# A decoder layer on one core: GpSimd's first row pass is moved behind the latents' inverse root and woven with weight splits, and three more weight loads stand ahead of it

## The chip, the cores and the metric

The kernel runs on one core of a Trainium2 chip. The metric is the device time of one execution in microseconds (us); lower is better. Engines are named as in the profile: PE is TensorE, PEld its weight loads, DVE is VectorE, ACT is ScalarE, POOL is GpSimd, SP is SyncE, which issues the DMAs.

## The reference

One post-norm decoder layer over 1024 tokens of width 1024, in float32. What this case touches is the start: the embedding LayerNorm and the first products with `w_in`.

```python
x = layer_norm(x, emb_ln_g, emb_ln_b)
proj = x @ w_in[l]
u_pool, q, c, iq, ik, iw = jnp.split(proj, SPLIT_POINTS, axis=-1)
pooled = causal_multiscale_pool(u_pool)
c = rms_norm(c, kv_norm_g[l])
o_lat = dsa_sparse_attention(q_lat, c, iq, ik, iw, rel_bias)   # indexer scores, top 256 keys, softmax
mix = jnp.concatenate([pool_out, attn_out], axis=-1) @ w_o[l]
x = layer_norm(ALPHA * x + mix, ln1_g[l], ln1_b[l])            # the residual is the normalized x
```

The normalized x is needed twice: transposed, as the operand of `w_in`, and by rows (with gain and bias), as the residual of the sum after the attention.

## The kernel before

All tokens are worked in two chunks of 512 (four blocks of 128 rows each, tile `rows`). Every product is exact to float32 by three passes: an operand is split in a high part (rounded to fp32r) and a low part (what is left), and PE adds high x high, low x high and high x low (lines 1427, 1428, 1429). The transposed x of a chunk is in `xhi` and `xlo`.

Weights come in units of 128 rows by 1024 columns. Unit n is loaded by SP into `wring[n % 4]`; ACT makes its high part `whi[n % 2]` (line 1133), as soon as PE is done with unit n - 2; POOL or DVE makes the low part `wlo[n % 2]` (`split_lo`, line 397); then PE multiplies. The units of chunk 0 are, in order, 0 ik, 1 c, 2 to 5 iq0 to iq3 (all split by DVE), and 6 to 9 u0 to u3, 10 to 13 q0 to q3 (split by POOL). SP may load unit n only when the low part of unit n - 4 is done, since both lie in one slot of the ring (line 415).

The order of each engine's work is written out by hand, and engines wait for one another by counting semaphores. What matters here:

- POOL: the rows' affine pass, `emb_gains` (lines 628 and 629): each of four blocks is multiplied by the gain and then gets the bias, and counts up `emb_rows`. Then `latents_inverse_rms` (lines 693 and 694), which waits for ACT's four sums of squares and which ACT waits for ahead of `lat_val`. Then the low parts of u0 to q1, and then, between the low parts of q2 and q3, the inverse roots for chunk 1 (lines 681 and 683), which wait for DVE's statistics.
- SP, one queue in program order: after the first loads, units 4 to 6; then it waits for each `emb_rows` and writes that block to memory (line 482); waits until all four are written; loads the x of chunk 1 over them (line 485); writes and reads back the bias rows (lines 488 and 490); then the units from 7 on.
- DVE: `x_lo` (lines 558 and 563), the low parts of c and iq0, `keys_queries_lo` (lines 588, 589, 599, 600, with the low parts of iq1 to iq3 between), then for each u unit the pooling (lines 529 to 548), for each unit two score sums (lines 859 and 863), and from the fourth unit on a block's statistics and normalization of chunk 1 (lines 814 to 828). After that comes `select_pair`, the top-k of two blocks (lines 879 to 890).
- ACT: for each unit `hi_after`, the high part of the unit two further on, and behind it in its queue the evacuation of this unit's product and two `relu_dots`. PE: the product of each unit (24 groups of matmuls of 512 columns) and two `dot`s; the first dot waits for the low parts of all four iq products.

Of the kernel before, what the change touches and what calls it, by code (L numbers as in the profile page):

```python
# [134 lines left out]
def layer(nc, x, emb_ln_g, emb_ln_b, rel_bias, w_in, pool_w, pool_scale, kv_norm_g, w_uk, w_uv, w_o,  # L135
# [15 lines left out]
    with ExitStack() as ctx:  # L151
# [195 lines left out]
        units = []  # L347
# [6 lines left out]
        U = {name: n for n, name in enumerate(units)}  # L354
# [37 lines left out]
        def split_lo(eng, name, sem_lo, at=None):  # L392

            n = U[name]

            eng.wait_ge(hi_ready, n + 1 if at is None else at)
            eng.tensor_tensor(parts_of(name, wlo[n % 2]), parts_of(name, wring[n % 4]),  # L397
                              parts_of(name, whi[n % 2]).bitcast(F32), ALU.subtract).then_inc(sem_lo, 1)
# [10 lines left out]
        def _(sp):  # L409
            def load_unit(name):  # L410
                n = U[name]
                slot = wring[n % 4]
                if n >= 4:

                    sp.wait_ge(*LO[units[n - 4]])
                if name[0] == "wo":
                    _, c, nh, u = name
                    sp.dma_start(k_pairs(slot), wod[:, 2 * u:2 * u + 2, nh * 512:nh * 512 + 512]).then_inc(ring_in[n % 4], 16)
                elif name[0] == "ik":

                    sp.dma_start(parts_of(name, slot), wind[:, :, COL_IK:COL_IK + KEYW]).then_inc(ring_in[n % 4], 16)
                else:
                    col = {"c": COL_C, "iq": COL_IQ, "q": COL_Q, "u": COL_U}[name[0]] + (P * name[2] if name[0] != "c" else 0)
                    sp.dma_start(k_columns(slot), wind[:, :, col:col + P]).then_inc(ring_in[n % 4], 16)

            def load_gains(g, b):
                sp.dma_start(gains[:, 0, :], g.to_broadcast([P, D])).then_inc(gains_in, 16)
                sp.dma_start(gains[:, 1, :], b.to_broadcast([P, D])).then_inc(gains_in, 16)
# [27 lines left out]
            def load_units(names):  # L456
                for name in names:
                    load_unit(name)
# [16 lines left out]
            sp.dma_start(wuv[:, :], w_uv.rearrange("o c h d -> (o c) (h d)")).then_inc(late_in, 16)  # L475
            sp.dma_start(poolw[:, :, :], pool_w.rearrange("o g c d -> c (o g) d")).then_inc(late_in, 16)
            load_gains(emb_ln_g.rearrange("(o d) -> o d", o=1), emb_ln_b.rearrange("(o d) -> o d", o=1))
            load_units(units[4:7])

            for b in range(CB):  # L480
                sp.wait_ge(emb_rows, b + 1)
# [2 lines left out]
            for b in range(CB):  # L484
# [4 lines left out]
            sp.wait_ge(bias_out, 16)  # L489
            sp.dma_start(near_up[:, :, :], bass.AP(tensor=bias_rows.tensor, offset=0, ap=[[1, P], [FWIN, HEADS], [1, NEAR]])  # L490
                         ).then_inc(bias_in, 16)
            load_units(units[7:U[("wo", 0, 1, 0)]])
            for b in range(CB):
                sp.wait_ge(emb_rows, CB + b + 1)
                sp.dma_start(spilld[CB + b], rows[:, b, :]).then_inc(spilled, 16)
# [127 lines left out]
        def emb_gains(eng, c, link):  # L623

            eng.wait_ge(gains_in, 32)
            eng.wait_ge(g_full, G[("xT", c, KT - 1)] + 1)
            for b in range(CB):
                link(eng.tensor_tensor(rows[:, b, :], rows[:, b, :], gains[:, 0, :], ALU.mult))
                eng.tensor_tensor(rows[:, b, :], rows[:, b, :], gains[:, 1, :], ALU.add).then_inc(emb_rows, 1)
                yield b  # L630
# [13 lines left out]
        def _(pool):  # L644
# [32 lines left out]
            def inverse_std(l, blocks=range(CB)):  # L677
                for b in blocks:
                    n = 4 * l + b
                    pool.wait_ge(stats_ready, n + 1)  # L680
                    pool.tensor_scalar(rstd[:, n:n + 1], mean_var[:, n, 1:2], EPS, None, ALU.add).then_inc(var_eps, 1)
                    pool.wait_ge(var_eps, n + 1)
                    pool.tensor_tensor(rstd[:, n:n + 1], rstd[:, n:n + 1], power[:, :], ALU.pow).then_inc(rstd_ready, 1)
                    if l in (LN1_0, LN1_1) or (l == LN2_1 and b in OUT_SHARED):
                        pool.wait_ge(rstd_ready, n + 1)
                        pool.tensor_scalar(shift[:, n:n + 1], mean_var[:, n, 0:1], rstd[:, n:n + 1], -1.0, ALU.mult, ALU.mult)\
                            .then_inc(shift_ready, 1)

            def latents_inverse_rms(c):
                at = slice(CB * c, CB * c + CB)  # L690

                pool.wait_ge(csum_ready, CB * c + CB)
                link(pool.tensor_scalar(crstd[:, at], csum[:, at], 1.0 / LAT, EPS, ALU.mult, ALU.add))
                pool.tensor_tensor(crstd[:, at], crstd[:, at], power[:, :].to_broadcast([P, CB]), ALU.pow)\
                    .then_inc(crstd_ready, 1)
# [38 lines left out]
            def lo(*names):  # L734
                for name in names:
                    split_lo(pool, name, lo_pool)

            inverse_std(EMB0)
            for b in emb_gains(pool, 0, link):
                pass  # L740
            latents_inverse_rms(0)
            lo(*units[U[("u", 0, 0)]:U[("q", 0, 2)]])

            inverse_std(EMB1, [0])
            lo(("q", 0, 2))
# [959 lines left out]
```

## Time and profile before

| what | value |
|---|---|
| median of 3 runs | 1308.09 us (1307.64 to 1311.28) |
| span of the profiled execution | 1309.0 us |
| PE busy | 1223.0 us (93%) |
| DVE busy | 869.9 us (66%) |
| ACT busy | 578.9 us (44%) |
| POOL busy | 539.0 us (41%) |

The page gives the profiled execution's span and no other time of it. The span is 0.9 us over the median of the three runs and inside their range. Busy shares are means over the whole program; the change lies in the first 130 us, where three engines hand work to one another, so the rows below are from there.

### The profile page before, as it was taken

The numbers are of one execution on the slowest core, as the hardware profiler recorded it, in microseconds if no ns is written. First come the engines' busy times: TensorE is split into PE (matmuls) and PEld (weight loads), VectorE is DVE, ScalarE is ACT, GpSimd is POOL, SyncE is SP. The second block draws the span as 40 slices with busy tenths as digits, with TensorE's granted clock in tenths as the row PEclk, the third lists the DMA queues.
The fourth block names the chain that finished last, engine by engine and source line by source line (L and its number), as shares of the span: only waits on it lengthen the run. The fifth ranks groups of instructions, "written<-read, shape, count | busy, mean of one in ns | idle before, by whom it ended". The sixth has DMA issues, their size and how long they took to land.

```text
span 1309.0 us, 17244 instructions
## 1 busy us (share of the span) xinstructions
PE 1223.0 (93%) x5639; PEld 981.3 (75%) x5639; DVE 869.9 (66%) x1322; ACT 578.9 (44%) x961; POOL 539.0 (41%) x390
## 2 busy tenths in 40 slices
PE   4999898799979999999999999989899999999994
PEld 2786685577868778778778698877688888888883
DVE  7577999765879888888888679833842232322345
ACT  3445642675564334243343376642542442433420
POOL 5434674422248666666665733214801102002004
PEclk9899999899989999999999999999799999999997
DMA  6722232131123232332322200403123323223331
GB/s 195 241 74 64 65 81 96 43 119 33 28 70 97 83 101 90 95 96 96 93 87 93 96 1 34 161 17 81 49 98 96 96 96 95 89 90 95 96 96 64
DMA packets 125723, 114.28 MB, mean 87 GB/s; under 512 B 5662, under 2 KB 99435, under 8 KB 125675
## 3 DMA queue, kind: packets, MB, share of 16 engines
q1 hardware_dynamic: 125674, 113.67, 28.0%
q8 instruction: 27, 0.44, 0.1%
q14 instruction: 22, 0.17, 0.0%
HBM read 105.25 MB, written 8.40 MB: 87 GB/s over the span
## 4 chain that ended last, share of the span: by engine, by line
PE 75%; DVE 14%; issue 6%; ACT 2%; POOL 1%; DVEq 1%; DMA 0%; ACTq 0%; POOLq 0%
PE g_bank L1427 14%; PE g_bank L1428 13%; PE g_bank L1429 13%; PE wide L1427 10%; PE wide L1429 10%; PE wide L1428 10%; PE g_bank L1401 2%; DVE logit L924 1%; DVE xlo L563 1%; DVE win L533 1%; PE wide L1530 1%; PE wide L1490 1%; PE wide L1489 1%; DVE probs_lo L940 1%; DVE score L863 1%
## 5 line engine op out<-in xcount | busy, mean ns | idle before, releaser
L397 POOL TENSOR_TENSOR wlo<-wring,whi 128x1024 fp32r<-128x1024 f32 (+1 forms) x102 | 252.4, 2476 | 274.1 <-ACT whi L1133 161.2
L1427 PE MATMUL g_bank<-xhi,whi 128*128 128x512 f32 (+1 forms) x736 | 298.5, 406 | 8.6 <-DVE xlo L563 5.8
L1313 ACT ACTIVATE whi<-wring 128x1024 fp32r<-128x1024 f32 x124 | 131.4, 1059 | 392.9 <-PE wide L1429 198.1
L1428 PE MATMUL g_bank<-xlo,whi 128*128 128x512 f32 (+1 forms) x736 | 294.5, 400 | 0.0
L1429 PE MATMUL g_bank<-xhi,wlo 128*128 128x512 f32 (+1 forms) x736 | 294.2, 400 | 0.0
L397 DVE TENSOR_TENSOR wlo<-wring,whi 128x1024 fp32r<-128x1024 f32 (+1 forms) x70 | 96.6, 1382 | 224.6 <-ACT whi L1313 220.0
L1427 PE MATMUL wide<-whi,hhi 128*128 128x512 f32 x512 | 202.7, 396 | 0.0
L1429 PE MATMUL wide<-whi,hlo 128*128 128x512 f32 x512 | 202.2, 395 | 0.0
L1428 PE MATMUL wide<-wlo,hhi 128*128 128x512 f32 x512 | 202.2, 395 | 0.0
L1427 PEld LDWEIGHTS g_bank<-xhi,whi 128*128 128x128 f32 (+1 forms) x736 | 139.7, 190 | 49.4 <-DVE xlo L563 7.8
L1429 PEld LDWEIGHTS g_bank<-xhi,wlo 128*128 128x128 f32 (+1 forms) x736 | 139.5, 190 | 35.0 <-issue 0.7
L732 POOL TENSOR_TENSOR rows<-rows,y_stage 128x512 f32<-128x512 f32 x56 | 72.6, 1318 | 226.2 <-ACT y_stage L1305 224.9
L1428 PEld LDWEIGHTS g_bank<-xlo,whi 128*128 128x128 f32 (+1 forms) x736 | 139.6, 190 | 34.7 <-issue 1.6
L908 DVE MAX8 top<-work 128x8 f32<-128x640 f32 (+3 forms) x128 | 131.6, 1028 | 18.7 <-DVE work L911 0.2
L911 DVE MATCH_REPLACE8 work<-top,work 128x640 f32<-128x640 f32 (+3 forms) x128 | 129.2, 1009 | 0.0
L1427 PEld LDWEIGHTS wide<-whi,hhi 128*128 128x128 f32 x512 | 96.0, 187 | 24.6 <-POOL wlo L397 1.3
L1429 PEld LDWEIGHTS wide<-whi,hlo 128*128 128x128 f32 x512 | 96.0, 187 | 23.4
L1428 PEld LDWEIGHTS wide<-wlo,hhi 128*128 128x128 f32 x512 | 96.0, 187 | 23.4
L1133 ACT ACTIVATE whi<-wring 128x1024 fp32r<-128x1024 f32 (+1 forms) x48 | 49.9, 1043 | 129.0 <-PE g_bank L1429 124.3
L723 POOL TENSOR_TENSOR mask<-score,near_bias 128x256 f32<-128x256 f32 (+1 forms) x64 | 44.7, 699 | 78.3 <-DVE row_max L924 68.6
L924 DVE CUSTOM_DVE_ANT_0 logit<-wide,mask 128x128 f32<-128x128 f32 (+7 forms) x64 | 48.3, 755 | 31.3 <-PE g_bank L1401 25.5
L1231 ACT ACTIVATE logit<-logit,neg_max 128x128 f32<-128x128 f32 (+7 forms) x64 | 49.7, 777 | 40.8 <-DVE neg_max L928 40.2
(183 smaller groups left out, 1928.6 us busy)
## 6 DMA issues: line engine op xcount, KB each, us to landing
wring<-in_w_up SPq DMA_DIRECT2D x64, 512.0 KB, 4.2
wring<-in_w_down SPq DMA_DIRECT2D x64, 512.0 KB, 3.5
wring<-in_w_in SPq DMA_DIRECT2D x26, 512.0 KB, 3.9
wring<-in_w_o SPq DMA_DIRECT2D x16, 512.0 KB, 3.5
rows<-in_x SPq DMA_DIRECT2D x8, 512.0 KB, 5.3
normalized_rows<-rows SPq DMA_DIRECT2D x8, 512.0 KB, 4.0
rows<-normalized_rows SPq DMA_DIRECT2D x8, 512.0 KB, 6.6
out<-rows SPq DMA_DIRECT2D x7, 512.0 KB, 2.7
```

What stands on the lines that cost most here:

```text
L397: eng.tensor_tensor(parts_of(name, wlo[n % 2]), parts_of(name, wring[n % 4]), parts_of(name, whi[n % 2]).bitcast(F32), ALU.subtract).then_ ...
L723: pool.tensor_tensor(mask[:, m % 2, length - near:length], score[:, i % CB, length - near:length], near_bias[:, h, NEAR - near:NEAR], ALU. ...
L732: pool.tensor_tensor(piece, piece, y_stage[:, b, :], ALU.add).then_inc(y_added, 1)
L908: nc.vector.max(top8[:, 0, :], w).then_inc(topk_steps, 1)
L911: nc.vector.match_replace(w, top8[:, 0, :], w, TAKEN).then_inc(topk_steps, 1)
L924: nc.vector.tensor_tensor_reduce(logit[:, m % 2, 0:length], wide[m % 2][:, 0:length], mask[:, m % 2, 0:length], 1.0, TAKEN, ALU.add, ALU.m ...
L1133: nc.scalar.activation(parts_of(name, whi[n % 2]), parts_of(name, wring[n % 4]), ACT.Copy).then_inc(hi_ready, 1)
L1231: nc.scalar.activation(p, p, ACT.Exp, bias=neg_max[:, m % 2:m % 2 + 1], accum_out=exp_sum[:, i % 2, h:h + 1]).then_inc(exp_ready, 1)
L1313: nc.scalar.activation(whi[(first + j) % 2][:, :], wring[(first + j + 2) % 4][:, :], ACT.Copy)\
L1427: nc.tensor.matmul(out_ap, w_hi, m_hi, start=first, stop=False)
L1428: nc.tensor.matmul(out_ap, w_hi, m_lo, start=False, stop=False)
L1429: return nc.tensor.matmul(out_ap, w_lo, m_hi, start=False, stop=last)
```

## The change

In POOL's program the latents' inverse root now stands first, then the row pass of blocks 0 and 1, then the low part of u0, block 2, the low part of u1, block 3, and the low parts of u2, u3, q0 and q1. In SP's program units 7, 8 and 9 are loaded ahead of the blocks' writes and of all that stands behind these; unit 10 is the first one after. Nothing else differs, and the same instructions are issued in all.

```diff
@@ -475,7 +475,7 @@
             load_gains(emb_ln_g.rearrange("(o d) -> o d", o=1), emb_ln_b.rearrange("(o d) -> o d", o=1))
-            load_units(units[4:7])
+            load_units(units[4:10])
@@ -489,7 +489,7 @@
-            load_units(units[7:U[("wo", 0, 1, 0)]])
+            load_units(units[10:U[("wo", 0, 1, 0)]])
@@ -736,10 +736,15 @@
             inverse_std(EMB0)
-            for b in emb_gains(pool, 0, link):
-                pass
             latents_inverse_rms(0)
-            lo(*units[U[("u", 0, 0)]:U[("q", 0, 2)]])
+            first_gains = emb_gains(pool, 0, link)
+            next(first_gains)
+            next(first_gains)
+            lo(("u", 0, 0))
+            next(first_gains)
+            lo(("u", 0, 1))
+            next(first_gains)
+            lo(*units[U[("u", 0, 2)]:U[("q", 0, 2)]])
```

POOL's order from the end of `inverse_std(EMB0)` on, before. `rows` is the chunk, `gains` gain and bias, and `wlo0<-wring2,whi0` is the low part of u0:

```order
L628 TENSOR_TENSOR rows<-rows,gains 128x1024 [waits g_full,gains_in]
L629 TENSOR_TENSOR rows<-rows,gains 128x1024 [waits pool_steps]
L628 TENSOR_TENSOR rows<-rows,gains 128x1024
L629 TENSOR_TENSOR rows<-rows,gains 128x1024 [waits pool_steps]
...
L693 TENSOR_SCALAR crstd<-csum 128x4 [waits csum_ready]
L694 TENSOR_TENSOR crstd<-crstd,power 128x4 [waits pool_steps]
L397 TENSOR_TENSOR wlo0<-wring2,whi0 128x1024 [waits hi_ready]
L397 TENSOR_TENSOR wlo1<-wring3,whi1 128x1024 [waits hi_ready]
```

The same place after:

```order
L693 TENSOR_SCALAR crstd<-csum 128x4 [waits csum_ready]
L694 TENSOR_TENSOR crstd<-crstd,power 128x4 [waits pool_steps]
L628 TENSOR_TENSOR rows<-rows,gains 128x1024 [waits g_full,gains_in]
L629 TENSOR_TENSOR rows<-rows,gains 128x1024 [waits pool_steps]
...
L397 TENSOR_TENSOR wlo0<-wring2,whi0 128x1024 [waits hi_ready]
L628 TENSOR_TENSOR rows<-rows,gains 128x1024
L629 TENSOR_TENSOR rows<-rows,gains 128x1024 [waits pool_steps]
L397 TENSOR_TENSOR wlo1<-wring3,whi1 128x1024 [waits hi_ready]
```

The eight row instructions now stand behind the wait for `csum_ready`, and four of them also behind a wait for a high part.

SP's queue at the same stage, before. `wring2` in the first row is unit 6 (u0), the last three rows are units 7, 8 and 10:

```order
L424 DMA wring2<-in_w_in 128x8x128 [waits lo_dve]
L482 DMA normalized_rows<-rows 128x1024 [waits emb_rows] x4
L485 DMA rows<-in_x 128x1024 [waits spilled]
L488 DMA bias_rows<-bias_row_64 8x384 [waits bias_row_ready]
L490 DMA near_up_61<-bias_rows 128x8x256 [waits bias_out]
L424 DMA wring3<-in_w_in 128x8x128 [waits lo_dve]
L424 DMA wring0<-in_w_in 128x8x128 [waits lo_dve]
...
L424 DMA wring2<-in_w_in 128x8x128 [waits lo_pool]
```

And after, where the three units stand ahead and `wring2` with `lo_pool` is unit 10 (q0):

```order
L424 DMA wring3<-in_w_in 128x8x128 [waits lo_dve]
L424 DMA wring0<-in_w_in 128x8x128 [waits lo_dve]
L424 DMA wring1<-in_w_in 128x8x128 [waits lo_dve]
L482 DMA normalized_rows<-rows 128x1024 [waits emb_rows] x4
L485 DMA rows<-in_x 128x1024 [waits spilled]
L488 DMA bias_rows<-bias_row_64 8x384 [waits bias_row_ready]
L490 DMA near_up_61<-bias_rows 128x8x256 [waits bias_out]
L424 DMA wring2<-in_w_in 128x8x128 [waits lo_pool]
```

The load of q0 is now the first one behind the four blocks and the bias rows, where u1's was.

## Rows read from the trace of the kernel before

**Rows 1.** The page: span, and the shares of the chain that ended last.

```profile
span 1309.0 us, 17244 instructions
PE 75%; DVE 14%; issue 6%; ACT 2%; POOL 1%; DVEq 1%; DMA 0%; ACTq 0%; POOLq 0%
```

**Rows 2.** Timeline of DVE: start us, us, engine, line, operation, count, [idle before].

```profile
22.81 4.91 DVE L563 TENSOR_TENSOR xlo<-val,xhi 128x512 fp32r<-128x512 f32 x2
30.41 6.68 DVE L397 TENSOR_TENSOR wlo<-wring,whi 128x1024 fp32r<-128x1024 f32 x2
...
58.56 0.69 DVE L599 TENSOR_TENSOR iq<-val,iq 64x512 fp32r<-64x512 f32 x1 [3.85 <-ACT iq L1170]
60.00 1.22 DVE L397 TENSOR_TENSOR wlo<-wring,whi 128x1024 fp32r<-128x1024 f32 x1
```

**Rows 3.** Timeline of POOL, 20 to 56 us.

```profile
21.98 2.41 POOL L628 TENSOR_TENSOR rows<-rows,gains 128x1024 f32<-128x1024 f32 x1 [9.11 <-PE g_bank L1401]
24.47 2.70 POOL L629 TENSOR_TENSOR rows<-rows,gains 128x1024 f32<-128x1024 f32 x1
...
42.20 2.71 POOL L629 TENSOR_TENSOR rows<-rows,gains 128x1024 f32<-128x1024 f32 x1
54.12 0.64 POOL L693 TENSOR_SCALAR crstd<-csum 128x4 f32<-128x4 f32 x1 [9.21 <-ACT squares L1181]
54.84 1.03 POOL L694 TENSOR_TENSOR crstd<-crstd,power 128x4 f32<-128x4 f32 x1
```

**Rows 4.** Timeline of PE, 25 to 74 us.

```profile
25.61 0.40 PE L1429 MATMUL g_bank<-xhi,wlo 128*72 128x512 f32 x1
27.77 0.45 PE L1427 MATMUL g_bank<-xhi,whi 128*72 128x512 f32 x1 [1.76 <-DVE xlo L563]
...
33.84 0.79 PE L1427 MATMUL g_bank<-xhi,whi 128*128 128x512 f32 x1 [1.74 <-DVE wlo L397]
...
42.16 0.60 PE L1401 MATMUL g_bank<-ident,wuk_raw 128*128 128x128 f32 x4
...
61.28 0.50 PE L1427 MATMUL g_bank<-xhi,whi 128*128 128x512 f32 x1
...
73.03 0.33 PE L1489 MATMUL wide<-key_hi,iq 128*128 128x384 f32 x1
```

**Rows 5.** Windows: stretch, length, PE, PEld, DVE, ACT, POOL busy, PEclk, DMA share, GB/s.

```profile
34.00:39.50 5.50, 5.50 (x13) 4.29 (x14) 5.50 (x2) 0.80 (x2) 5.42 (x3) 0.50 0.56 132
90.00:100.00 10.00, 10.00 (x44) 7.89 (x43) 9.45 (x17) 4.13 (x7) 2.75 (x1) 1.00 0.32 81
```

**Rows 6.** The chain that ended last, 19 to 204 us: start us, us, what.

```profile
40.69 0.23 PE g_bank L1429
...
105.37 0.35 POOL rstd L681
...
109.32 0.50 PE g_bank L1427
...
201.38 0.76 DVE work L890 x2
```

**Rows 7.** Timeline of SP's queue, 47 to 57 us.

```profile
47.56 1.77 SPq L485 DMA_DIRECT2D rows<-in_x  x4
...
55.11 1.80 SPq L424 DMA_DIRECT2D wring<-in_w_in  x2
```

**Rows 8.** DMA issues, 55.05 to 55.5 us: the load of u1, and its time to landing.

```profile
wring<-in_w_in SPq DMA_DIRECT2D x1, 512.0 KB, 6.9
```

**Rows 9.** Tile wring, SP alone, 50 to 125 us.

```profile
DMA to landing us min/median/max: 3.0/3.8/8.1
```

**Rows 10.** Timeline of ACT: the high part of q0.

```profile
85.90 1.06 ACT L1133 ACTIVATE whi<-wring 128x1024 fp32r<-128x1024 f32 x1 [4.00 <-PE g_bank L1429]
```

**Rows 11.** Timeline of DVE, 89 to 127 us.

```profile
89.78 0.16 DVE L529 COPY uT<-hist 128x16 f32<-128x16 f32 x1
...
126.37 4.05 DVE L879 COPY work<-score 128x384 f32<-128x384 f32 x2 [0.18 <-POOL score L702]
```

## The prediction

> **What bounds the kernel now.** I read the page first. By its chain PE has 75% of the span and DVE 14% [rows 1], so whether a change in the first 130 us reaches the end depends on who is last there. The chain runs, in turn, through DVE, PE, DVE again, and at 105 us from DVE's statistics over POOL's inverse root and the low part of q2 to PE's product of q2 at 109.32 [rows 6]. At 126.37 DVE begins the top-k of two blocks [rows 11], and from there the chain stays on DVE until after 201 us [rows 6]. So what moves the start of the top-k at 126.37 moves the end by the same amount, and I work out that one start.
>
> Then the timelines of DVE and POOL, side by side. From 21.98 to 44.91 POOL does the row pass, eight instructions [rows 3], and in this stretch DVE's instructions are three times as long as they are elsewhere: two `xlo` took 4.91 and two low parts of weights 6.68, while one such low part alone took 1.22 and half an iq low part 0.69 [rows 2]. The starts and ends fit one rule: each engine waits for the other's whole instruction, then takes its turn. The first row instruction ended at 24.39, the next ended at 27.17, and the DVE pair that had asked at 22.81 ended at 27.72, one turn after each [rows 2, 3]. A turn of POOL holds DVE for about 2.2 us (27.17 less 24.39, less DVE's 0.6). PE waits for these low parts: it has the sixth part of ik done at 25.84, waits till 27.77, waits again, and starts the product of c at 33.84 [rows 4]. After these gaps its granted clock is 0.50, the lower of the two levels (1.2 against 2.4 GHz): 13 matmuls in 5.5 us, 0.42 us each [rows 5], where 0.23 (0.2335 over a long run of them) is the step at the full clock [rows 6].
>
> **The change, step 1: what it frees (9.3 us).** With POOL idle until the sums of squares, DVE's pair ends at about 24.1, `xlo` 7 at 25.8 and the low part of c at 27.0. PE does not stop: six more matmuls after 25.84 end at 27.25, and c takes 24 x 0.2335 = 5.6, to 32.85. Before, c ended at 42.16 [rows 4]. All that follows is 9.3 earlier, as far as it hangs on PE. The inverse root of the latents itself gains nothing by standing first, since the row pass had been over for 9.21 us when it started [rows 3].
>
> **Step 2: the same row pass, later, beside DVE's iq low parts (takes 9.7 back).** The inverse root starts at 54.12 - 9.3 = 44.8 and takes 1.75 with its second instruction [rows 3], so the row pass starts at 46.6. Turn by turn: POOL to 49.0 and to 51.5; DVE's half of iq1, asked at 58.56 - 9.3 = 49.3, ends at 52.1; POOL to 54.3; the other half to 54.9; POOL to 57.1; the low part of unit iq3 (1.1) to 58.2. PE wants that at 61.28 - 9.3 = 52.0 [rows 4]. Of 9.3 us, 3.1 are left. PE has then been idle for 6 us, longer than any of the gaps behind which it was at the lower clock; I take the same 5.7 us at that clock as from 33.84 to about 39.5, which costs 5.7 x (1 - 0.2335/0.42) = 2.5. The product of iq3 ends at 66.4, where it was 67.1. Next is u0, and its dots wait for all iq low parts. ACT has evacuated iq3 at about 69.3; POOL does the low part of u1 to 70.0, DVE the first half to 70.6, POOL a row instruction to 72.8, DVE the second to 73.4. The first dot starts at 73.4; it was 73.03 [rows 4]. The whole 9.3 is gone, and 0.4 more. The low parts of u0, u1 and u2 are ready when PE wants them: u0's, for one, is done at about 61, and PE comes to it at 66.9.
>
> **Step 3: the load of q0 (costs 6.8).** The last row instruction ends at 75.6 (three more turns after 70.6: 72.8, DVE, 75.6); before it was 44.91 [rows 3]. SP is one queue: the x of chunk 1 was issued 2.65 behind it, at 47.56, and u1's load 7.55 later, at 55.11 [rows 7], with the write of the bias rows and its landing between. Now q0 stands in u1's place: issued at 75.6 + 2.65 + 7.55 = 85.8. Behind the x and the bias rows u1's load took 6.9 to land [rows 8]; over the stretch such loads took 3.0 to 8.1, most 3.8 [rows 9]. I take 6.9, since what is in front of it is the same: 92.7. ACT wants q0 at 85.90 [rows 10] (its instruction then waited for PE alone). So it stalls for 6.8, and behind its wait stand the evacuation of u2 and two relus. DVE's pooling of u2, at 89.78 [rows 11], comes 6.8 later. From 90 to 100 DVE is 9.45 of 10 us busy [rows 5], so its statistics for chunk 1 come 6.8 later, and by the chain over POOL's inverse root at 105.37 and q2's low part so does PE's q2 at 109.32 [rows 6]. The units before could hide a PE delay of a few us; this chain hides none. The top-k starts at 133.2.
>
> The bounds of the landing are 3.0 and 8.1: the stall is 2.9 to 8.0. The three loads put ahead cost nothing: they waited for DVE's low parts only and are over before the first block is written; they gain nothing either, since u1 and u2 were never what ACT waited for.
>
> By the Trainium skill, DMA: Bandwidth & Descriptors, sections Specifications and Anatomy of one DMA, a transfer has some 2 us of fixed cost and memory gives one core about 358 GB/s. From these figures, as an estimate, 1 MB of bias rows and 0.5 MB of q0 land together 6.4 us after the first issue, 6.0 after q0's, and the sum would be +5.9. The row with the measured 6.9 decides.
>
> **The sum.** 0 from steps 1 and 2 as far as ACT's wait is concerned (PE is 0.4 late, which the load covers), + 6.8 from step 3. On the profiled span 1309.0 + 6.8 = 1315.8; on the median, which is 0.9 lower, 1308.1 + 6.8 = 1314.9.
>
> **The rivals.**
> A, one of the two costs is absent. If DVE and POOL don't hold each other in the new place, POOL runs without turns: blocks 0 and 1 to 56.4, u0's low part, block 2, u1's, block 3 to 71.0, and q0 lands at 71.0 + 17.1 = 88.1, 2.2 late: 1310.3. If q0 is there in time but the turns are as I have them, the 0.4 of step 2 is left: 1308.5. For it: DVE has gaps here, 3.85 before iq1's half [rows 2]. Against: nothing in the rows shows a DVE instruction with two inputs pass a POOL one. Both are no measurable change.
> B, the other side: both are absent, the front's gain stays. Then only POOL's blocks 2 and 3 delay the low parts of u1 (ready at 66.1, wanted after the two dots, at 73.7 - 9.3 = 64.4, so 1.7) and u2 (about 1.0): 9.3 - 2.7 = 6.6 faster, 1301.5. It decides if POOL's rows end before about 66 and PE's iq3 starts at 52.
> C, slower still: after the stall PE has several gaps of 2 to 3 us (before dot 6, before q2), as it had at 26 to 34, and falls to the lower clock once more, on the chain at q2. That adds 2.5: 1317.4.
>
> The rule of the Trainium skill that speaks against this change is in GPSIMD Engine Reference, section Specifications: GpSimd shares its SBUF interfaces with VectorE, and instructions with two SBUF inputs contend. By it, moving the pass moves the collision and does not end it. The trace agrees by [rows 2]; that it holds in the new place too is what A denies.
>
> **How the numbers follow.** My forecast 0.60, C 0.14, A 0.17, B 0.09. What a measurement of this kernel can tell from no change is 0.3%, 3.9 us: slower means over 1312.0. The forecast's own range, from the landing's bounds with 1 us for the turns, is 1310 to 1317; a part of it, some 0.05, and A are within 0.3%. With C inside and most of A the range is 1308.5 to 1318.8. Faster 0.08, same 0.20, slower 0.72.
>
> **What would show it.** Step 1: no idle PE from 25.8 to 33, c over at about 33, granted clock 1.0 there. Step 2: DVE's L599, L600 and L397 of 2 to 3 us between 49 and 59, and a PE gap of about 6 us ahead of iq3 with the lower clock behind it. Step 3: x of chunk 1 issued at about 78, q0's load at 86, an ACT wait of about 7 us for a landing at line 1133, the top-k beginning at about 133. The prediction is wrong if ACT's high part of q0 still waits for PE, or if the top-k begins before 130 us.

## The result and the profile after

The changed kernel takes 1318.26 us (median of 4 runs, 1317.21 to 1321.5) against 1308.0 (1307.64 to 1311.28) for the one before on the same chip: ratio 1.0068, with the interval [1.0053, 1.0082], which is 8.9 us. The two medians themselves stand 10.3 us apart, a ratio of 1.0078, which lies inside that interval; what follows goes by 1.0068. The predicted time was 1314.9, so the sign and the mechanism came as forecast and the size 2.1 us short of that ratio, 3.4 short of the median. The two profiled executions differ by 6.4 us.

The page of the changed kernel answers to [rows 1]:

```profile
span 1315.4 us, 17244 instructions
PE 76%; DVE 13%; issue 6%; ACT 3%; POOL 1%; DVEq 1%; DMA 0%; SPq 0%; ACTq 0%; POOLq 0%
```

The shares tell nothing of 6 us in 1315. What answers is the timeline of DVE after the change (start us, us, engine, line, operation, count, [idle before]); lines behind the edit in POOL's program stand 5 further down than before:

```profile
22.95 1.29 DVE L563 TENSOR_TENSOR xlo<-val,xhi 128x512 fp32r<-128x512 f32 x2
...
28.70 1.23 DVE L397 TENSOR_TENSOR wlo<-wring,whi 128x1024 fp32r<-128x1024 f32 x1 [1.48 <-ACT whi L1138]
...
49.37 2.70 DVE L599 TENSOR_TENSOR iq<-val,iq 64x512 fp32r<-64x512 f32 x1 [3.85 <-ACT iq L1175]
52.10 2.72 DVE L600 TENSOR_TENSOR iq<-val,iq 64x512 fp32r<-64x512 f32 x1
54.86 3.25 DVE L397 TENSOR_TENSOR wlo<-wring,whi 128x1024 fp32r<-128x1024 f32 x1
...
70.55 2.78 DVE L600 TENSOR_TENSOR iq<-val,iq 64x512 fp32r<-64x512 f32 x1
```

Against [rows 2], two `xlo` fell from 4.91 to 1.29, and an iq low part rose from 0.69 to 2.7. The collision has moved from the low parts of x and c to those of iq. POOL's timeline shows the other partner of these turns:

```profile
46.63 2.41 POOL L628 TENSOR_TENSOR rows<-rows,gains 128x1024 f32<-128x1024 f32 x1
49.12 2.40 POOL L629 TENSOR_TENSOR rows<-rows,gains 128x1024 f32<-128x1024 f32 x1
51.48 2.79 POOL L628 TENSOR_TENSOR rows<-rows,gains 128x1024 f32<-128x1024 f32 x1
54.35 2.68 POOL L629 TENSOR_TENSOR rows<-rows,gains 128x1024 f32<-128x1024 f32 x1
```

PE, against [rows 4]: the timeline no longer has a wait between 25 and 33, and has one of 5.95 us ahead of iq3. Behind it the windows (stretch, length, busy time of PE, PEld, DVE, ACT and POOL, PEclk, DMA share, GB/s) show 0.56 over 6 us, most of it at the lower level:

```profile
58.17 0.80 PE L1432 MATMUL g_bank<-xhi,whi 128*128 128x512 f32 x1 [5.95 <-DVE wlo L397]
...
73.47 0.41 PE L1494 MATMUL wide<-key_hi,iq 128*128 128x384 f32 x1 [1.12 <-DVE iq L600]
```

```profile
26.00:33.00 7.00, 7.00 (x32) 5.27 (x31) 3.81 (x5) 2.61 (x4) 0.00 (x0) 1.00 0.58 150
...
58.00:64.00 6.00, 5.83 (x15) 4.68 (x16) 5.90 (x4) 0.00 (x0) 5.92 (x3) 0.56 0.75 246
```

SP's queue, which answers to [rows 7], and the two instructions of ACT and DVE that follow from it:

```profile
58.55 17.38 SPq L482 DMA_DIRECT2D normalized_rows<-rows  x4
78.24 1.76 SPq L485 DMA_DIRECT2D rows<-in_x  x4
...
85.91 6.73 SPq L424 DMA_DIRECT2D wring<-in_w_in  x4
```

```profile
92.82 1.06 ACT L1138 ACTIVATE whi<-wring 128x1024 fp32r<-128x1024 f32 x1 [10.42 <-DMA wring<-in_w_in]
```

```profile
94.39 1.96 DVE L529 COPY uT<-hist 128x16 f32<-128x16 f32 x1 [6.22 <-ACT uT L1113]
...
132.70 4.05 DVE L884 COPY work<-score 128x384 f32<-128x384 f32 x2 [0.18 <-POOL score L702]
```

ACT's high part of q0, at 85.90 behind PE in [rows 10], now starts at 92.82 behind the landing of its weights. Of these 6.9 us 6.36 arrive at the inverse root (111.73, it was 105.37), and 6.32 at PE's q2 (115.64, it was 109.32) [rows 6]; by what way is told under step 3 below:

```profile
111.73 0.35 POOL rstd L681
...
115.64 0.50 PE g_bank L1432
```

The top-k begins at 132.70, 6.33 later than at 126.37 [rows 11]. From there to the end of the span it is 1182.7 us, and was 1182.6: the whole difference of the profiled executions was made before the top-k.

### The profile page after: what moved, and what is told of

It is laid out like the page before. It is cut to its first block, busy times and chain, and to the rows that moved or that the text cites. A ratio compares the mean times of both kernels' runs of the same rounds, so it can differ in the third digit from the quotient of the medians.

```text
span 1315.4 us, 17244 instructions
## 1 busy us (share of the span) xinstructions
PE 1224.4 (93%) x5639; PEld 982.2 (75%) x5639; DVE 870.5 (66%) x1322; ACT 578.4 (44%) x961; POOL 537.6 (41%) x390
## 4 chain that ended last, share of the span: by engine, by line
PE 76%; DVE 13%; issue 6%; ACT 3%; POOL 1%; DVEq 1%; DMA 0%; SPq 0%; ACTq 0%; POOLq 0%
PE g_bank L1432 14%; PE g_bank L1433 14%; PE g_bank L1434 14%; PE wide L1432 10%; PE wide L1434 10%; PE wide L1433 10%; PE g_bank L1406 2%; DVE logit L929 1%; DVE win L533 1%; PE wide L1494 1%; PE wide L1495 1%; PE wide L1535 1%; DVE probs_lo L945 1%; DVE xlo L563 1%; DVE work L895 1%
## 5 line engine op out<-in xcount | busy, mean ns | idle before, releaser
L397 DVE TENSOR_TENSOR wlo<-wring,whi 128x1024 fp32r<-128x1024 f32 (+1 forms) x70 | 93.1, 1331 | 227.9 <-ACT whi L1318 220.0
```

## The experiments

Each was timed against the kernel before, on its own chip. "Top-k" is the start of DVE's two copies of `score`, as in [rows 11].

**The changed kernel once more.** No edit; a second profile.

> The changed kernel again, for the size of the loss. The first time its four runs stood 0.68% above before, 8.9 us, where the two profiled spans differ by 6.4 and the starts of the top-k by 6.3. Theory: over more runs the loss is 6.3 to 7.5 us, ratio 1.0048 to 1.0057, and the rest was which executions met long and which short. Rival: about 9 us again, so that another 2 to 3 us are lost after the top-k's start, and the stretch from that start to the end is longer than in the kernel before by as much.

Measured: 1319.36 us (6 runs, 1317.52 to 1320.35) against 1311.09 (11 runs), ratio 1.0068 [1.0056, 1.0080]; span 1317.6, top-k at 134.94. The loss is the same by the ratio, over the 6.3 to 7.5 us that I had expected and as the rival had it, but not where the rival put it. In this execution the top-k is 8.6 later than in [rows 11], and 2.2 later than in the first profile of the changed kernel. The rest of the span is 1182.7 again, so what was more than 6.3 came ahead of the top-k. Windows and ACT's timeline of this execution say where it began:

```profile
21.00:23.00 2.00, 1.67 (x6) 1.40 (x7) 1.66 (x4) 1.76 (x4) 0.00 (x0) 0.50 0.48 139
23.00:25.00 2.00, 2.00 (x7) 1.15 (x6) 1.69 (x3) 1.67 (x3) 0.00 (x0) 0.66 0.01 4
```

```profile
29.06 1.06 ACT L1138 ACTIVATE whi<-wring 128x1024 fp32r<-128x1024 f32 x1 [3.60 <-PE g_bank L1434]
...
95.05 1.06 ACT L1138 ACTIVATE whi<-wring 128x1024 fp32r<-128x1024 f32 x1 [10.94 <-DMA wring<-in_w_in]
```

In the first profile both windows had a granted clock of 1.00 and ACT's instruction behind ik stood at 27.61. Here the clock was 0.50 and 0.66 in the product of ik, that instruction came 1.45 later, and q0's high part 2.23 later.

**The kernel before once more.** No edit.

> The kernel before, unchanged, for a second profile of it. The two profiled spans differ by 6.4 us (1309.0 and 1315.4), the medians by 10.3. Theory: the first profile of before fell on one of its longer executions; a second has a span of 1305.5 to 1307, and the extra 2 to 3 us show in one stretch as matmuls at the lower clock. Rival: the span is 1309 again and what lies around it is smaller for the kernel before.

Measured: 1309.11 us (10 runs, 1308.30 to 1311.22), ratio 1.0000 [0.9991, 1.0010]; span 1307.3, top-k at 125.93, with 1181.4 behind it. So top-k and span agree between these two executions to 0.4 and 1.7 us. The span is just over the theory's, but its explanation was wrong: the first and longer execution had the full clock in ik. Why it was the longer one is not shown. It is this one that had the lower clock there:

```profile
21.00:23.00 2.00, 1.92 (x7) 1.58 (x8) 1.66 (x3) 1.97 (x3) 0.67 (x1) 0.52 0.40 123
```

```profile
32.17 1.06 ACT L1133 ACTIVATE whi<-wring 128x1024 fp32r<-128x1024 f32 x1 [5.09 <-PE g_bank L1429]
```

ACT's instruction behind ik stands at 32.17; in the first profile of the kernel before, at clock 1.00, it stood at 32.20. Where PE waited for held low parts anyway, the slower PE cost nothing.

**The loads alone.** POOL's order of before, three units ahead:

```diff
-            load_units(units[4:7])
+            load_units(units[4:10])
...
-            load_units(units[7:U[("wo", 0, 1, 0)]])
+            load_units(units[10:U[("wo", 0, 1, 0)]])
```

> The change's queue part alone: units 7 to 9 are loaded ahead of the blocks' writes, POOL's order is as before. My theory (the price lies in the load of q0 behind a late row pass): the last of the three loads waits for the low part of iq3 at 61.2 us, the x of chunk 1 is issued at about 65 and the load of q0 at about 72, landing at 79, ahead of 85.9 where ACT wants it. So no change, within 0.3% (1304 to 1312), top-k starting within 0.5 us of 126.4. Rival (the longer SP queue itself, or the transfers colliding, costs): slower by 2 us or more, with an ACT wait for a landing at the high part of q0 or q1.

Measured: 1309.80 us (12 runs, 1308.29 to 1313.18) against 1309.84 (29 runs), ratio 1.0002 [0.9992, 1.0011]; top-k at 126.39. The three loads cost nothing and bring nothing. SP's queue and ACT:

```profile
61.23 3.39 SPq L482 DMA_DIRECT2D normalized_rows<-rows  x4
70.55 1.76 SPq L485 DMA_DIRECT2D rows<-in_x  x4
...
79.25 2.14 SPq L424 DMA_DIRECT2D wring<-in_w_in  x2
```

```profile
86.19 1.06 ACT L1133 ACTIVATE whi<-wring 128x1024 fp32r<-128x1024 f32 x1 [4.72 <-DMA wring<-in_w_in]
```

One number was a miss: the x of chunk 1 followed the writes after 9.3 us, where I had expected the small distance of the other kernels. There the first three blocks had long been written when the fourth was queued; here all four (2 MB) were queued together, right behind a weight load. It left q0's load at 79.25, and ACT waits for its landing, but at 86.19 it is only 0.3 later than behind PE [rows 10]. An issue at 79 is thus about the last one that costs nothing: the kernel before had slack in SP's queue, and this one has used it up.

**The loads alone, with the writes held back.** The kernel above with one wait more in SP's program, for the low part of u1, which stands where POOL has done about as much as at the changed kernel's last block:

```diff
             load_units(units[4:10])
+            sp.wait_ge(*LO[("u", 0, 1)])
             for b in range(CB):
```

> POOL's order as in the kernel before and units 7 to 9 ahead (which alone made no difference), but SP writes the blocks only when the low part of u1 is done, at 70.8 instead of 61.2 us. So the load of q0 is late and nothing else is: no row pass stands in a new place. It is issued at about 88.8 and lands at about 95.5. My theory (a late q0 load is paid one to one, by the chain over the statistics and q2's low part): ACT waits 9.5 us for the landing, top-k at 135.9 to 136.5, ratio 1.0068 to 1.0078. Rival (PE and DVE have 3 to 6 us of slack in the units from u3 to q3, and hide as much): ratio 1.0025 to 1.005, top-k at 130 to 133.

Measured: 1319.34 us (6 runs, 1314.42 to 1321.13), ratio 1.0066 [1.0049, 1.0084]; top-k at 134.13, about 2 earlier than expected, since the four blocks, queued at 71.80, let x go at 78.76, after 7.0 us and not the 9.3 of the kernel above. SP and ACT of this kernel:

```profile
78.76 1.76 SPq L486 DMA_DIRECT2D rows<-in_x  x4
...
87.22 1.82 SPq L424 DMA_DIRECT2D wring<-in_w_in  x2
```

```profile
94.23 1.06 ACT L1134 ACTIVATE whi<-wring 128x1024 fp32r<-128x1024 f32 x1 [11.36 <-DMA wring<-in_w_in]
```

Against the loads alone, q0's load was issued 8.0 later, ACT's high part came 8.0 later, and the top-k 7.7 later. POOL's order is that of before, the row pass stands where it stood, and the loss is that of the changed kernel (with q0's load issued 1.3 later than in its first profile): step 3 is enough for it. The x of chunk 1 and the bias rows are late here too. That they are not the cause is shown by the next kernel, where they are later still.

**The changed kernel with q0 ahead too.** Step 3 taken away, steps 1 and 2 left:

```diff
-            load_units(units[4:10])
+            load_units(units[4:11])
...
-            load_units(units[10:U[("wo", 0, 1, 0)]])
+            load_units(units[11:U[("wo", 0, 1, 0)]])
```

> The whole change, and one load more (unit 10, q0) ahead of the blocks' writes. My theory: step 3 goes and steps 1 and 2 stay. PE still idles about 6 us ahead of iq3 at 52 to 58, ACT's high part of q0 waits for PE again, at about 85.5, and the top-k starts at 126.1 to 126.8 (it was 132.7 with the change, 126.4 before). 6.2 us below the changed kernel, within 0.3% of the kernel before. Rival A (the loss is the turns between DVE and POOL, the late load is hidden by them): at most 2 us below the changed kernel. Rival B (q1's load, now the first behind the bias rows, takes the wait over): top-k at 129 or later.

Measured: 1310.57 us (11 runs, 1309.48 to 1313.14), ratio 1.0008 [0.9999, 1.0017]; top-k at 128.65. The loss is gone but for 0.8 thousandths, and nothing of step 1's 9.3 us is seen. PE and ACT:

```profile
59.53 0.80 PE L1432 MATMUL g_bank<-xhi,whi 128*128 128x512 f32 x1 [5.95 <-DVE wlo L397]
```

```profile
88.14 1.06 ACT L1138 ACTIVATE whi<-wring 128x1024 fp32r<-128x1024 f32 x1 [4.00 <-PE g_bank L1434]
```

The gap of 5.95 is there to the hundredth, so step 2 is independent of the load, and ACT waits for PE again, for q0 and for q1 (at 95.30), so rival B's wait for the load of q1 is not there. The x of chunk 1 was issued at 79.96, 1.7 later than in the changed kernel's first profile, at no visible cost. The top-k came 1.8 to 2.5 later than expected: this execution had the lower clock in ik (0.53 and 0.61), and ACT's instruction behind ik stood at 28.98.

**The pass left out.** POOL leaves out the affine pass of chunk 0 (the residual of the first 512 tokens is then without gain and bias) and only counts up `emb_rows`; all else as before.

```diff
-            for b in emb_gains(pool, 0, link):
-                pass
+            pool.wait_ge(gains_in, 32)
+            pool.wait_ge(g_full, G[("xT", 0, KT - 1)] + 1)
+            pool.sem_inc(emb_rows, CB)
```

> Order and queue of the kernel before, but the affine row pass of chunk 0 is left out (the residual of the first 512 tokens lacks gain and bias); POOL counts up emb_rows when the transposes are done. The full price of the pass. My theory by the turns: c over at 32.9, iq3 at 51.9, top-k at 116 to 117, 9.5 us below before: ratio 0.9925 to 0.993. Rival (DVE's long instructions in 22 to 46 us are slow for another reason, as the DMA traffic of the weights): top-k at 123 or later, ratio 0.997 or more.

Measured: 1301.38 us (4 runs, 1300.20 to 1303.11), ratio 0.9930 [0.9915, 0.9944]; top-k at 117.35, 9.0 earlier than before. This is what the pass costs in the kernel before, and the most that placing it elsewhere can give. Step 1 had 9.3. DVE's low part of c took 1.22 in this kernel and that of iq0 1.22, so the rival (DVE is slow there because of the weights' DMA traffic) is ruled out: the loads are the same.

**The pass in DVE's idle time.** In the changed kernel DVE idles for 7.2 us ahead of iq0's low parts and for 3.9 ahead of iq1's. Here POOL waits for the low part of iq1, then does blocks 0 and 1, the inverse root, block 2, u0's low part, block 3. The diff is against the changed kernel, with q0's load ahead as above:

```diff
-            latents_inverse_rms(0)
             first_gains = emb_gains(pool, 0, link)
+            pool.wait_ge(*LO[("iq", 0, 1)])
             next(first_gains)
             next(first_gains)
-            lo(("u", 0, 0))
+            latents_inverse_rms(0)
             next(first_gains)
-            lo(("u", 0, 1))
+            lo(("u", 0, 0))
             next(first_gains)
-            lo(*units[U[("u", 0, 2)]:U[("q", 0, 2)]])
+            lo(*units[U[("u", 0, 1)]:U[("q", 0, 2)]])
```

> A new place for the row pass: POOL waits for DVE's low part of iq1 (34.4 to 35.6 in the changed kernel), does blocks 0 and 1, the latents' inverse root, block 2, u0's low part, block 3, then the low parts of u1 on; q0's load ahead of the blocks' writes. DVE is idle for 7.2 us from 35.6 and for 3.9 from 45.5 in the changed kernel, so half of the turns hold nobody. My theory by the turns: iq3 starts at 54.3, the first dots at about 70, the top-k at 119 to 120, 6.5 to 7 us below the kernel before: 1301.5. Rival (each row instruction costs its turn wherever it stands): top-k at 125 or later, no change against before.

Measured: 1305.96 us (5 runs, 1303.73 to 1307.27), ratio 0.9965 [0.9952, 0.9978]; top-k at 122.07, some 2 to 3 later than expected. Of step 1's gain 4.3 us stay. DVE and PE show two remnants:

```profile
43.50 2.78 DVE L600 TENSOR_TENSOR iq<-val,iq 64x512 fp32r<-64x512 f32 x1
```

```profile
47.59 0.50 PE L1432 MATMUL g_bank<-xhi,whi 128*128 128x512 f32 x1 [1.05 <-DVE wlo L397]
...
55.44 0.50 PE L1432 MATMUL g_bank<-xhi,whi 128*128 128x512 f32 x1 [1.98 <-DVE wlo L397]
```

Block 1's add runs past the end of the idle time and holds a low part for 2.1 us; block 2 does the same to iq1's low parts. After the second gap the clock was 0.79 and 0.65 over 6 us.

**The pass beside the low parts that nobody waits for.** POOL waits for the low part of c and does three blocks; then the inverse root; waits for the low part of iq3; then block 3. Again against the changed kernel, with q0's load ahead:

```diff
-            latents_inverse_rms(0)
             first_gains = emb_gains(pool, 0, link)
+            pool.wait_ge(*LO[("c", 0)])
             next(first_gains)
             next(first_gains)
-            lo(("u", 0, 0))
             next(first_gains)
-            lo(("u", 0, 1))
+            latents_inverse_rms(0)
+            pool.wait_ge(*LO[("iq", 0, 3)])
             next(first_gains)
-            lo(*units[U[("u", 0, 2)]:U[("q", 0, 2)]])
+            lo(*units[U[("u", 0, 0)]:U[("q", 0, 2)]])
```

> The row pass placed by the rule of turns: POOL waits for the low part of c (27 us), does blocks 0, 1 and 2, the latents' inverse root, waits for the low part of iq3, does block 3, then the low parts from u0 on; q0's load ahead of the blocks' writes. Between 27 and 42 DVE has only five instructions, and PE wants what they make some us later than they are ready. My theory by the turns: PE runs without a gap through c, iq0, iq1 and iq2, iq3 starts at about 52 and the top-k at 117.6 to 119; 7.5 to 8.5 us below the kernel before, ratio 0.9935 to 0.9945. Rival (what the row pass costs does not depend on its place, the 0.35% of the run before was all there is): ratio 0.996 or more, with new PE gaps of over 1 us ahead of iq1 or iq2.

Measured: 1305.07 us (6 runs, 1304.39 to 1306.19) against 1311.09 (11 runs), ratio 0.9961 [0.9949, 0.9973]; top-k at 120.68. The gain is real but under the expected one, and the ratio is the rival's (0.996 or more); but the gaps ahead of iq1 and iq2 that the rival needed are not there. DVE between 33 and 43, and PE's only gap that is left:

```profile
33.45 2.87 DVE L588 TENSOR_TENSOR key_lo<-val,key_hi 64x512 fp32r<-64x512 f32 x1
36.35 2.78 DVE L589 TENSOR_TENSOR key_lo<-val,key_hi 64x512 fp32r<-64x512 f32 x1
39.16 3.31 DVE L397 TENSOR_TENSOR wlo<-wring,whi 128x1024 fp32r<-128x1024 f32 x1
```

```profile
61.62 0.50 PE L1432 MATMUL g_bank<-xhi,whi 128*128 128x512 f32 x1 [1.44 <-POOL wlo L397]
```

Three DVE instructions are held here as hard as any, and PE does not stop for them: the keys' low parts are wanted only by the first dot, and iq1's low part was not due. The one gap is for u0's low part, which stood behind block 3. And this execution had the lower clock in ik (0.61 and 0.53), with ACT behind ik at 29.42.

**Block 3 behind u0's low part.** The kernel above without the wait for iq3:

```diff
             latents_inverse_rms(0)
-            pool.wait_ge(*LO[("iq", 0, 3)])
+            lo(("u", 0, 0))
             next(first_gains)
-            lo(*units[U[("u", 0, 0)]:U[("q", 0, 2)]])
+            lo(*units[U[("u", 0, 1)]:U[("q", 0, 2)]])
```

> The early row pass once more, with u0's low part ahead of block 3 and no wait for iq3's. In the run before PE waited 1.44 us for u0's low part (61.62), which stood behind block 3. My theory: this wait goes; the top-k starts 1 to 1.5 us earlier than there if PE's product of ik meets the same clock (about 119.3 with the lower clock at 21 to 25 us, 118 without), ratio to before 0.994 to 0.9955. Rival (block 3's two instructions now hold DVE's iq low parts, for which the first dot waits, by as much): no difference to 0.9961.

Measured: 1305.61 us (10 runs, 1302.68 to 1307.28) against 1309.19 (18 runs), ratio 0.9969 [0.9959, 0.9978]; top-k at 121.01. It is no better than the kernel above, as the rival had it, though its profiled execution had the clock at 1.00 in ik. DVE, PE and two windows:

```profile
56.82 2.78 DVE L600 TENSOR_TENSOR iq<-val,iq 64x512 fp32r<-64x512 f32 x1
...
62.44 2.75 DVE L599 TENSOR_TENSOR iq<-val,iq 64x512 fp32r<-64x512 f32 x1
```

```profile
66.06 0.41 PE L1494 MATMUL wide<-key_hi,iq 128*128 128x384 f32 x1 [1.82 <-DVE iq L600]
```

```profile
66.00:68.00 2.00, 1.94 (x8) 1.77 (x9) 2.00 (x1) 0.87 (x2) 2.00 (x1) 0.85 0.71 225
68.00:70.00 2.00, 2.00 (x6) 1.52 (x5) 1.83 (x6) 0.00 (x0) 0.15 (x1) 0.50 1.01 352
```

The wait for u0's low part is gone and one for the last iq low part, 0.4 longer and followed by the lower clock, stands in its place. One gap was traded for another.

**The same with filler for PE in ik.** Eight more transposes of `ident` into a bank that is free, to keep PE busy between ik's parts:

```diff
+                    for _ in range({5: 2, 6: 2, 7: 4}.get(k, 0) if (what, c) == ("xT", 0) else 0):
+                        nc.tensor.transpose(wide[0][:, 0:P], ident[:, :], ident[:, :])
```

> The same kernel with eight more transposes of the identity on PE, into a bank that is free there, two ahead of the transposes k = 5 and 6 and four ahead of k = 7 (17 to 21 us), where PE otherwise has gaps. In five of ten profiles PE's granted clock is at the lower level from 21 to 25 us, after these gaps, and the product of ik then ends some 1.45 us later (the high part of iq0 at 29.0 to 29.4 us in place of 27.6 to 27.75). Theory: with the gaps filled the clock stays at its upper level in all executions; against the kernel without them the median falls by 0.7 to 1.4 us and the executions lie closer together; in the profile the high part of iq0 starts at 27.6 to 28.2. Rival (the gaps have nothing to do with it, or the extra transposes delay the real ones by as much): the same or up to 0.5 us slower.

Measured: 1305.84 us (9 runs, 1304.64 to 1307.52), ratio 0.9976 [0.9967, 0.9986]; top-k at 121.73. The clock in ik was 1.00, as it was in one execution without the fillers; ACT's instruction behind ik stood at 28.02, 0.67 later than there. The times show no gain. Whether the fillers keep the clock up stays open: one profile of each can't tell it, and what they might give they also take. PE was busy for the whole of 17 to 19 us here, and for 1.54 of it in the kernel without them, which kept the clock in ik as well; the executions that lost it had less, as the last section says.

The start of the top-k and the span, over all profiled executions:

| kernel | top-k | span | span less top-k |
|---|---|---|---|
| before / once more | 126.37 / 125.93 | 1309.0 / 1307.3 | 1182.6 / 1181.4 |
| changed / once more | 132.70 / 134.94 | 1315.4 / 1317.6 | 1182.7 / 1182.7 |
| loads alone / writes held back | 126.39 / 134.13 | 1310.5 / 1316.8 | 1184.1 / 1182.7 |
| q0 ahead too | 128.65 | 1308.8 | 1180.2 |
| pass left out | 117.35 | 1301.3 | 1184.0 |
| pass in DVE's idle time | 122.07 | 1305.5 | 1183.4 |
| pass beside low parts not due | 120.68 | 1304.3 | 1183.6 |
| block 3 behind u0 / with filler | 121.01 / 121.73 | 1302.2 / 1303.0 | 1181.2 / 1181.3 |

The last column lies between 1180.2 and 1184.1 over starts from 117.35 to 134.94, and has no slope with the start that shows over this scatter.

## Why the prediction was right, and where its size was off

**That the start of the top-k is the one number to work out** held: the table above. It also sets the limit of every comparison of two single profiles here: 2.2 us in the start of the top-k (the changed kernel's two), and in what lies behind it up to 3.9 over all kernels.

**Step 1, c over at 32.85 and no idle PE.** In the first profile of the changed kernel the last matmul of c starts at 32.74 and ACT's instruction behind c at 33.23; the clock over 26 to 33 was 1.00. The pass left out gives 9.0 for the same 9.3. This is also the term that was mis-sized, for the time if not for that profile. I had read the front of ik from one execution at the full clock and taken the kernel after for the same. In five of the twelve profiled executions the clock in ik was between 0.50 and 0.66 (each kernel that was profiled twice had one of either). In the kernel before that costs nothing, since PE waits for DVE behind it (32.17 against 32.20); in the changed kernel it costs 1.45 at once and 2.2 at the top-k (134.94 against 132.70). So step 1's gain is 9.3 in one kind of execution and about 7.9 in the other, and the turns of step 2, the blocks and q0's load start that much later. How much of the missing 2.1 us this is can only be estimated: 6.3 us and, in 5 of 12 executions, 2.2 more make 7.3 on the mean, at the low end of the interval's 6.9 to 10.7; if all had it, it would be 8.6. The unprofiled executions have no clock by rows, so the rest stays open. How the span stands to the time was also read wrongly: the profiled execution of the changed kernel has 1317.21 us for a span of 1315.4, so a time is 1.8 above its span, and a span of 1309.0 belongs to an execution of the kernel before of about 1310.8, not to one near its median. So the first pair of profiles set a long execution before (2.8 over the median) beside a short one after (1.0 under it), and these 3.8 are nearly all by which the medians' 10.3 exceeds the profiles' 6.4. The predicted difference isn't touched by that.

**Step 2, the turns.** Right in every row named here: POOL at 46.63, 49.12, 51.48, 54.35 where the working had 46.6, 49.0, 51.5 and 54.3 as bounds of turns; the low part of iq3 done at 58.1 (58.2), PE's gap 5.95 (6), the first dot at 73.47 (73.4), with the lower clock between. With q0's load out of the way the ratio is 1.0008 [0.9999, 1.0017]: 9.3 freed and 9.7 given back had been predicted as 0.4 late, 1.0003.

The Trainium skill, GPSIMD Engine Reference, section Specifications, has GpSimd and VectorE share SBUF interfaces, with contention for DVE instructions that have two SBUF inputs or run in a 2-port perf mode. By that the move could only carry the collision elsewhere. The rows agree, and show its size here, one whole instruction of the other engine: 2.7 us for a DVE instruction of 0.69.

**Step 3, the load.** x at 78.24 (78.25), q0's load at 85.91 (85.8), ACT at 92.82 (92.7). The load held back, with the row pass in its old place, gives 1.0066 [1.0049, 1.0084], and moving it ahead takes the loss away. The landing took 6.9 again, and 6.9 to 7.1 in the four profiles of kernels with a late q0 or the loads alone. The estimate in the prediction had 6.0 from the Trainium skill, DMA: Bandwidth & Descriptors; in the section Anatomy of one DMA the 2 us are given for a DMA that GpSimd issues, and these loads are SP's.

What followed the wait was not as worked out, though the sum came out nearly right. I had DVE's pooling of u2 6.8 later, and no slack. It began at 94.39, 4.6 later than at 89.78 [rows 11], since in the kernel before DVE was not waiting for ACT there: it was still at two score sums that POOL's low part of q0 held. DVE before:

```profile
86.36 3.50 DVE L863 SCALAR_TENSOR_TENSOR score<-relu_sb,idx_w,score 128x384 f32<-128x384 f32 x2
...
94.07 3.29 DVE L863 SCALAR_TENSOR_TENSOR score<-relu_sb,idx_w,score 128x384 f32<-128x384 f32 x2
...
103.76 0.69 DVE L814 BATCH_NORM_STATS2 stats<-rows 128x6 f32<-128x512 f32 x1
```

And after, where the copy at 94.39 (1.96, shown above) and one window sum are held instead:

```profile
97.31 2.61 DVE L533 TENSOR_TENSOR win<-win 128x526 f32<-128x526 f32 x1
...
110.12 0.69 DVE L819 BATCH_NORM_STATS2 stats<-rows 128x6 f32<-128x512 f32 x1
```

From the pooling to the statistics it is 13.98 us before and 15.73 after. The same two instructions are held in the kernel with the writes held back (1.96 and 2.60). So the 6.9 us on ACT were cut to 4.6 by slack in DVE, and two new collisions with POOL's low parts of q0 and q1, in place of one, gave 1.75 back: 6.36. That these two nearly cancel was luck, and "this chain hides none" was wrong.

**The rivals.** A needed DVE and POOL not to hold each other in the new place, or q0 in time; the rows rule out both. The second half of A was then built as a kernel, and its 1308.5 for a base of 1308.1 came as 1.0008. B needed both costs absent: taking away the load's gives 1.0008, and placing the pass so that both are small gives 0.9961, 5.1 us of its 6.6. C put a further lower clock at q2. PE had three gaps there (1.33, 1.38 and, before q2, 2.34), the chain's step from the inverse root to q2 is 3.91, where it was 3.95, and from q2 to the top-k it is 17.06, where it was 17.05: no such loss. Its number, 1317.4, was nearer to the measured 1318.26 than mine, and it is only by the room given to C that 1318.26 lies in the stated range: the forecast's own ended at 1317. That was luck too, since C's cause did not come about; what the runs show in its place, for a part, is the lower clock in ik.

## What to carry to other kernels

Work out what a moved pass will run beside, instruction by instruction, and count whole turns of the other engine; two places were better than the old one and the changed one: where DVE idles (0.9965), and beside instructions whose results are not due (0.9961, 0.9969). The runs do not tell these two apart; leaving the pass out gives 0.9930. Then follow every queue behind it: here a load of q0 issued at 79 cost nothing and one issued at 86 cost 6.3, not all of it by the wait: a late instruction meets other partners. Where a reordering uncovers an engine that was waiting, it uncovers that engine's own scatter too, so profile such a kernel twice before explaining 2 us.

## What the runs showed of the hardware

- A small DVE copy with one input is held by POOL as well: the copy of 128x16 at 94.39 took 1.96 us beside POOL's low part at 93.95, and 0.16 alone [rows 11]. Whether it ran in a 2-port perf mode, as the Trainium skill's rule above would have it, no view here shows. An evacuation from PSUM is not: in the kernel before, amid POOL's row pass of [rows 3], it took the 0.80 that it takes everywhere, between two instructions that were held:

```profile
27.64 0.80 DVE L558 TENSOR_SCALAR val<-g_bank,vecs 128x512 f32<-128x512 f32 x1
28.48 2.02 DVE L563 TENSOR_TENSOR xlo<-val,xhi 128x512 fp32r<-128x512 f32 x1
```

  The hold works the other way too: in the changed kernel POOL's low part at 56.99, begun while DVE's at 54.86 still ran, took 3.34, and 2.36 when it began first, at 93.95.
- TensorE's granted clock in the same stretch of the same kernel differs from one execution to the next: 1.00 or 0.50 (2.4 or 1.2 GHz) at 21 to 23 us, in the kernel before and in the changed one. In the changed kernel PE had been busy for 0.96 us of the 2 us before (19 to 21) in the execution that kept the clock, and for 0.95 in the one that lost it. The two differ one stretch earlier, at 17 to 19, in the first profile and in the second:

```profile
17.00:19.00 2.00, 1.54 (x8) 1.17 (x7) 1.91 (x4) 1.78 (x4) 0.00 (x0) 1.00 0.95 352
17.00:19.00 2.00, 1.18 (x8) 0.97 (x7) 1.91 (x4) 1.78 (x4) 0.00 (x0) 1.00 0.98 338
```

  In all five profiles that lost the clock PE was busy for less of this stretch than in any of the seven that kept it. That this is the cause is not shown.
- Four blocks of 512 KB, queued together to be written to memory, took 9.3 us from the first issue to the release of what waits for them with a weight load right in front (loads alone) and 7.0 without one (writes held back). When the first three had been queued long before, it was 2.65 from the end of the last block's POOL instruction [rows 3, 7].
